# Lower parts by an accumulating DMA in every second weight half, and the retention gate between the token tiles

## What is computed

```
h = rms_norm(x, norm1_w)
q, k, v, g_ret, x_lru, y_lru, gate_ret, gate_lru = split(h @ w_in)
o = chunkwise_retention(rotary(q), rotary(k), v)     # 4 heads of 256
mu, var over each head of o
o = (o - mu) * rsqrt(var + eps) * gn_w               # head_group_norm
y_a = (o * silu(g_ret)) @ w_ret_o
y_b = (rg_lru(conv(x_lru)) * gelu(y_lru)) @ w_lru_o
x = x + (sigmoid(gate_ret) * y_a + sigmoid(gate_lru) * y_b) @ w_out
h = rms_norm(x, norm2_w)
gate, val = split(h @ ffn_w_up)                      # 3072 each
x = x + (gelu(conv3(gate)) * val) @ ffn_w_down
out = rms_norm(x, norm_f_w)
```

## Time and profile before

| | us |
|---|---|
| median of 3 executions | 993.83 (992.47 to 996.0) |
| the profiled execution, its own time | 990.71 |
| its span, first to last instruction | 988.9 |
| TensorE busy in the span | 922.5 |
| GpSimd busy | 440.5, of which L2093 405.1 |
| VectorE busy | 445.3 |
| ScalarE busy | 333.4, of which L1026 139.3 |

### The profile page before, as it was taken

How to read it: one execution, slowest core, us unless ns; L and a number is a source line. 1 busy time by engine, 2 the same in 40 slices (tenths; PEclk the granted TensorE clock), 3 DMA queues, 4 the chain that set the end, 5 groups by cost and what they waited for, 6 DMA issues and landing times.

```text
span 988.9 us, 15018 instructions
## 1 busy us (share of the span) xinstructions
PE 922.5 (93%) x5878; PEld 834.1 (84%) x5878; DVE 445.3 (45%) x951; ACT 333.4 (34%) x636; POOL 440.5 (45%) x561
## 2 busy tenths in 40 slices
PE   4999999999999999999989997799999998999995
PEld 3888888888888776788989997798988998899894
DVE  2284475512588788713592366501122353232132
ACT  3102443102001144504444765243112443443441
POOL 0040000100011000006899689793450798999992
PEclk9999999999999899999999999799999999999998
DMA  8444223143343411332645355252523364555551
GB/s 336 157 149 150 86 86 121 54 157 137 129 170 129 171 43 44 104 124 85 220 144 172 105 198 170 85 188 88 221 75 129 108 190 156 172 185 191 173 189 44
DMA packets 37640, 139.35 MB, mean 141 GB/s; under 512 B 4289, under 2 KB 4289, under 8 KB 37313
## 3 DMA queue, kind: packets, MB, share of 16 engines
q1 hardware_dynamic: 37424, 136.97, 40.1%
q10 hardware_dynamic: 144, 1.41, 0.3%
HBM read 137.32 MB, written 1.05 MB: 140 GB/s over the span
## 4 chain that ended last, share of the span: by engine, by line
PE 65%; POOL 19%; DVE 9%; issue 3%; ACT 2%; DMA 2%; SPq 0%; DVEq 0%; ACTq 0%; POOLq 0%
PE psum L496 35%; POOL w_lo L2093 18%; PE psum L497 7%; PE psum L498 7%; PE psum L499 7%; PE psum L647 2%; PE psum L629 2%; PE psum L640 1%; PE psum L571 1%; DMA w_whole<-in_blocks 1%; DVE head_sums L1989 1%; DVE y_lo L1419 1%; DVE h_rows L1568 1%; PE psum L763 1%; ACT w_hi L1026 1%
## 5 line engine op out<-in xcount | busy, mean ns | idle before, releaser
L2093 POOL TENSOR_TENSOR w_lo<-raw,w_hi 128x256 fp32r<-128x256 f32 x536 | 405.1, 798 | 143.8 <-ACT w_hi L1026 142.8
L496 PE MATMUL psum<-w_whole,h_whole 128*128 128x256 f32 (+1 forms) x960 | 219.6, 382 | 1.9 <-ACT h_whole L1064 1.1
L497 PE MATMUL psum<-h_hi,w_hi 128*128 128x256 f32 x704 | 203.0, 288 | 17.9 <-DVE rows L1983 11.9
L2101 POOL TENSOR_TENSOR rstd<-mean_sq,minus_half 128x2 f32<-128x2 f32 (+4 forms) x20 | 35.1, 1753 | 399.6 <-DVE mean_sq L1429 399.6
L498 PE MATMUL psum<-h_lo,w_hi 128*128 128x256 f32 x704 | 201.7, 287 | 0.0
L499 PE MATMUL psum<-h_hi,w_lo 128*128 128x256 f32 x704 | 201.5, 286 | 0.0
L496 PEld LDWEIGHTS psum<-w_whole,h_whole 128*128 128x128 f32 x960 | 177.6, 192 | 26.5 <-issue 2.8
L1026 ACT ACTIVATE w_hi<-raw 128x1024 fp32r<-128x1024 f32 x136 | 139.3, 1054 | 95.2 <-DMA raw<-in_blocks 68.0
L497 PEld LDWEIGHTS psum<-h_hi,w_hi 128*128 128x128 f32 x704 | 137.6, 195 | 20.4 <-DVE rows L1983 12.1
L498 PEld LDWEIGHTS psum<-h_lo,w_hi 128*128 128x128 f32 x704 | 137.7, 196 | 0.1
L499 PEld LDWEIGHTS psum<-h_hi,w_lo 128*128 128x128 f32 x704 | 137.7, 196 | 0.0
(11 more groups left out here) (276 smaller groups left out, 1260.4 us busy)
## 6 DMA issues: line engine op xcount, KB each, us to landing
raw<-in_blocks SPq DMA_DIRECT2D x136, 512.0 KB, 3.5
w_whole<-in_blocks SPq DMA_DIRECT2D x96, 512.0 KB, 4.4
w_late<-in_blocks SPq DMA_DIRECT2D x20, 512.0 KB, 4.6
early<-in_early SPq DMA_DIRECT2D x1, 1651.0 KB, 7.4
attention<-in_late ACTq DMA_DIRECT2D x1, 1376.0 KB, 7.6
rows<-in_mem SPq DMA_DIRECT2D x2, 512.0 KB, 3.4
x<-in_x SPq DMA_DIRECT2D x1, 1024.0 KB, 9.5
out_x<-h_rows SPq DMA_DIRECT2D x2, 512.0 KB, 2.6
```

What stands on the lines that cost most here:

```text
L496: return nc.tensor.matmul(out, lhs[0], rhs[0], start=start, stop=stop, skip_group_check=shared_bank)
L497: nc.tensor.matmul(out, lhs[0], rhs[0], start=start, stop=False, skip_group_check=shared_bank)
L2093: ins = nc.gpsimd.tensor_tensor(lo[:, at], full[:, at], hi[:, at].bitcast(F32), ALU.subtract)
L2101: rstd_ready.mark(nc.gpsimd.tensor_tensor(rstd[:, n % 2, 0:width], mean_sq[:, n % 2, 0:width], minus_half[:, 0:width], ALU.pow), name, pool)
```

## The change

In every second half (odd j, except the last) the lower part is no longer subtracted by GpSimd. ScalarE writes the negated rounded weight into `w_lo` and the rounded weight into `w_hi`, both from `raw`. GpSimd issues, per quarter, a DMA that reads the quarter again from HBM and adds it onto `w_lo`, so that weight minus upper part stands there when it has landed (`lo_landed`, one semaphore for each quarter of each split slot). TensorE waits for `w_hi_ready` and the two landings instead of `w_lo_ready`. The `raw` slot of such a quarter is free once `w_hi_ready` has counted it. Halves 1, 3, ..., 65 are made so: 33 halves, 66 quarters.

In the retention part the separate scaling of `head_sums` goes: the mean is subtracted by one instruction per token tile that scales and adds. The two halves of the gate `g_ret1` are applied one after each of these instructions instead of both after the mean of the squares.

```
             else:
-                eng.wait_ge(w_lo_ready, 2 * (half_index[half] + 1))
+                j = half_index[half]
+                if lower_by_dma(j):
+                    eng.wait_ge(w_hi_ready, 2 * (j + 1))
+                    for q in (2 * j, 2 * j + 1):
+                        eng.wait_ge(*summed_at(q))
+                else:
+                    eng.wait_ge(w_lo_ready, subtracted(2 * j + 1))
+        def lower_by_dma(j):
+            return j % 2 == 1 and j < len(HALVES) - 2
...
             for q in range(2 * len(HALVES)):
-                if q >= RAW_SLOTS:
-                    sp.wait_ge(w_lo_ready, q - RAW_SLOTS + 1)
+                if q >= RAW_SLOTS and lower_by_dma((q - RAW_SLOTS) // 2):
+                    sp.wait_ge(w_hi_ready, q - RAW_SLOTS + 1)
+                elif q >= RAW_SLOTS:
+                    sp.wait_ge(w_lo_ready, subtracted(q - RAW_SLOTS))
...
                         act.wait_ge(quarter_landed[q % RAW_SLOTS], 16 * (q // RAW_SLOTS + 1))
+                        if lower_by_dma(j):
+                            if j < SPLIT_SLOTS:
+                                slot_left(act, 2 * j + 1)
+                            nc.scalar.activation(split_part(w_lo, q), raw[:, q % RAW_SLOTS, :], ACT.Copy, scale=-1.0)
                         nc.scalar.activation(split_part(w_hi, q), raw[:, q % RAW_SLOTS, :],
                                              ACT.Copy).then_inc(w_hi_ready, 1)
...
-            retention_gate(0)
+            for half in range(2):
+                retention_gate(0, half)
             for h in range(RET_HEADS):
                 settle(xpose, ("ret", h))
-            link(V.tensor_scalar(head_sums[:, :, :], head_sums[:, :, :], -1.0 / S, None, ALU.mult))
             o = h_rows[:, :, :].rearrange("p t (h d) -> p t h d", h=RET_HEADS)
             for t in range(T):
-                link(V.tensor_tensor(o[:, t], o[:, t], spread(head_sums[:, t, :], [P, RET_HEADS, S], 2), ALU.add))
+                link(V.scalar_tensor_tensor(o[:, t], spread(head_sums[:, t, :], [P, RET_HEADS, S], 2), -1.0 / S, o[:, t],
+                                            ALU.mult, ALU.add))
+                retention_gate(1, t)
...
-            r = scale_from("gn", sumsq[:, 0:T * RET_HEADS], S, between=lambda: retention_gate(1))
+            r = scale_from("gn", sumsq[:, 0:T * RET_HEADS], S)
...
                         pool.wait_ge(w_hi_ready, q + 1)
+                        if lower_by_dma(j):
+                            pool.dma_start(split_part(w_lo, q), blocks_d[2 * len(WHOLE) + q],
+                                           accum_op=ALU.add).then_inc(lo_landed[q % (2 * SPLIT_SLOTS)], 16)
+                            continue
```

More of the change, by code:

```diff
@@ L351, in build @@
         w_lo_last = sem("w_lo_last")
+        lo_landed = [sem(f"lo_landed{i}") for i in range(2 * SPLIT_SLOTS)]
         SRC = ([f"x2_{j}" for j in range(4)] + [f"ret_y{j}" for j in range(4)]
@@ L414, in wait_half, with subtracted, summed_at @@
             else:
-                eng.wait_ge(w_lo_ready, 2 * (half_index[half] + 1))
+                j = half_index[half]
[7 more added lines that the diff above has]
+            return j % 2 == 1 and j < len(HALVES) - 2
+        def subtracted(q):
+            return sum(not lower_by_dma(p // 2) for p in range(q + 1))
+        def summed_at(q):
+            turn = sum(lower_by_dma(j) for j in range(q // 2 % SPLIT_SLOTS, q // 2 + 1, SPLIT_SLOTS))
+            return lo_landed[q % (2 * SPLIT_SLOTS)], 16 * turn
         def split_part(w, q):
@@ L1436, in root_of, with scale_from @@
                 return rstd[0:p, n % 2, 0:NORMS[n][1]]
-            def scale_from(name, sums, count, factor=1.0, between=None):
+            def scale_from(name, sums, count, factor=1.0):
                 mean_from(name, sums, count, factor)
@@ L1446, in scale_from @@
                     angles()
-                if between is not None:
-                    between()
                 return root_of(name, sums.shape[0])
@@ L1974, in _, with retention_gate @@
                 decayed(h)
[L1976 to L1984, removed]
-            retention_gate(0)
+            def retention_gate(b, half):
+                n = 2 * b + half
+                use = (f"g_ret{b}", half)
+                arrive(proj, use)
+                vec.wait_ge(g_tanh, n + 1)
+                dst = rows[:, :, 2048 + 512 * b + HC * half:2048 + 512 * b + HC * (half + 1)]
+                proj.freed(V.scalar_tensor_tensor(dst, by_tokens(act_tmp[:, n % 2, :]), 1.0,
+                                                  by_tokens(bank_of(use)), ALU.add, ALU.mult), use, vec)
+            for half in range(2):
+                retention_gate(0, half)
             for h in range(RET_HEADS):
                 settle(xpose, ("ret", h))
-            link(V.tensor_scalar(head_sums[:, :, :], head_sums[:, :, :], -1.0 / S, None, ALU.mult))
             o = h_rows[:, :, :].rearrange("p t (h d) -> p t h d", h=RET_HEADS)
             for t in range(T):
-                link(V.tensor_tensor(o[:, t], o[:, t], spread(head_sums[:, t, :], [P, RET_HEADS, S], 2), ALU.add))
+                link(V.scalar_tensor_tensor(o[:, t], spread(head_sums[:, t, :], [P, RET_HEADS, S], 2), -1.0 / S, o[:, t],
+                                            ALU.mult, ALU.add))
+                retention_gate(1, t)
                 sq = scratch[:, :].rearrange("p (h d) -> p h d", d=S)
```

## The result

The changed kernel takes 1071.11 us (median of 4, 1069.95 to 1074.63) beside 993.15 for the kernel before: ratio 1.080, 95% interval 1.077 to 1.083. It is 78 us slower; the forecast was 17.7 us faster, with a range that ended at 1008. Rival (a), slow adding transfers, is what happened, at more than the price that it was given.

What follows compares the result with a forecast made beforehand. TensorE and GpSimd were taken to run at the same pace, 5.7 us a half. Retention -13.4, GpSimd's relief -12.7 and late DMA halves +8.4 gave -17.7 us, a median near 976, range 965 to 1008.

Steps and rivals of the forecast that it cites:

- Rival (a): Accumulating transfers are slow, TensorE waits in nearly every odd half, kernel slower; about 1033 us at x = 10.5; chance 0.22.
- What bounds the kernel: TensorE and GpSimd run at the same pace, 5.7 us a half; TensorE's waits for GpSimd are 8.4 us.
- The size of x: End of ScalarE's fourth copy to landing of the second quarter: taken as 5.2 us, making FFN halves 8.4 us late.
- The upper bound: Largest x allowed: 7.0 us, twice the 3.5 us plain load, if reading the destination too doubles everything.
- The formula around x: TensorE wants an odd half after 11.4 us; less eviction and copies, x may be 6.4 us, 3.8 in the tight half.
- the gains of 26.1 us: Time saved before DMA costs: 13.4 us in the retention part plus 12.7 us from relieving GpSimd.
- Share of the engines: DMA engines in the FFN: 84% at the plain price, 112% at twice it, then 38 us a step, about 997.
- Retention part: At the block 2 gate, TensorE's 12.1 us stand and 2.8 us of clock go, 1.5 us come back: 13.4 us less.
- Rival (c): VectorE's new scale-and-add is still held by GpSimd, at most 5.7 us; about 981 us; chance 0.12.
- GpSimd's relief: 33 of 67 halves leave GpSimd; TensorE's waits and low clock shrink, 4.9 us at 509-526 us and 7.8 in the FFN: 12.7 us.
- the signs named: Trace signs if right: GpSimd under 240 us busy, no gate wait, one 1 to 2 us wait per FFN step, landings 4 to 6 us.

Runs made afterwards that it cites:

- the copy run: The changed kernel with GpSimd's DMAs copying the quarter onto `w_lo` without adding: 1007.7 us, ratio 1.015.
- the sooner issue: Against the kernel summing only first quarters of odd halves by DMA, GpSimd issues on the negated copy instead of the upper part: 993.97 us, ratio 1.000.
- the DMA part alone: The changed kernel with the retention part of the kernel before: 1066.16 us, ratio 1.073.
- the retention run: The kernel before with only the retention part of the change, every lower part subtracted by GpSimd: 989.13 us, ratio 0.998.

## Why the prediction was wrong

**What bounds the kernel: right.** TensorE and GpSimd keep the same pace, and relieving GpSimd has little to give: 16 us for both parts with the transfers free.

**The size of x: the step that failed.** The prediction took x, from ScalarE's last copy to the landing, at 5.2 us between 3.5 and 7.0. It is 959.8 to 970.8, 11.0 us, in the chain shown; the second quarters land 9.9 us after their issue (median of 33, 5.8 to 11.8). The upper bound, twice the plain landing, was itself too low. By the medians three pieces are in it. A plain first quarter from GpSimd's queue lands in 4.8 us, against 3.5 on SyncE's queue in the kernel before: 1.3 us, of which the share of GpSimd's path and that of the other traffic were not separated. Adding puts 3.4 us on top, 8.2 instead of 4.8, which is inside the 1.6 to 3.5 that the prediction had for a second read; it is more than the engine time shows, which nearly doubles (312 against 163 ns a packet, some 1.3 us for the 144 packets over 16 engines). And the second quarter of a pair lands 1.8 us later after its issue than the first, as in the copy run (2.1 us): the quarters are issued 0.6 to 3.7 us apart, and the second shares the engines with the first. I priced one plain landing of SyncE's queue plus the second read, and neither of the other two pieces.

**The formula around x: right for pairs, too hopeful for single quarters.** The window of 11.4 us, minus copies and eviction, was stated, and with a measured chain of 15.1 us it gives 3.7 us of stand where 3.9 were measured. The rule behind (a stand is what the chain is over 11.4 us, shared between neighbours where every odd half is late) foretold two results: 17 us for a chain 1.05 us shorter (16 expected) and 1064 us for half the DMA halves (1055 to 1080 expected). With single quarters it was too hopeful three times: 996 us against 990, 994 against 981 to 984 with the sooner issue, and 1004 against 983 to 987 with ten of them. There GpSimd's own subtractions hold back many of the issues, which the rule leaves out, and a single quarter lands in 8 to 9 us. At x = 10.5 the rival gave 1033, 38 us under the result. What the sum left out or had too large points that way: x was nearer 11, the clock fell with the longer stands (up to 30 us), and the gains of 26.1 us were at most 16. How the 38 us divide between these was not measured.

**Share of the engines: wrong as a bound.** Rival (a) argued from 112% of the DMA engines. Over two FFN steps their share was 0.79, in a window within a stand 1.04 (as the profile counts it). That they fill up in spurts may lengthen a landing, which no run shows by itself; the halved traffic of the run with every fourth half shows that the sum was not the limit. Its step of 38 us was also short of the 44.6 measured. The rule of the Trainium skill, Collectives: The Full Stack, section The bandwidth ceiling, that an adding transfer reads two sources and runs at half the rate, agrees with the 1.85 of this trace, and with 1.91 against the plain packets of GpSimd's own queue. The fit of the Trainium skill, DMA: Bandwidth & Descriptors, section Anatomy of one DMA, an estimate of 3.2 us, does not cover what was seen: 5.4 us for the plain copy beside other traffic.

**Retention part: wrong by all its gain.** 13.4 us less were expected; alone it gave 0.2%, at most 0.4% or 4 us, and not clear of nothing. The step that failed is that the first scale-and-add takes 1.23 us from 606.06 on. 1.23 us was L1992 beside an idle GpSimd; beside a busy one it was held 11.26 us in the execution traced. Rival (c) had named it, but with a hold of at most one half's run, 5.7 us, on the ground that DMA halves break up GpSimd's runs. In the changed kernel they do (the scale-and-add took 1.31 us beside a run of eight pieces), but there the gain was worth nothing: with the DMA part alone the old order was not held either, 0.26 us, and TensorE did not wait for the gate line. The two gains were added up, though the second one took away what the first was to remove.

**GpSimd's relief: mechanism right, size not separated.** 12.7 us was the sum. Without transfers the FFN has no stand left, as foretold, and both parts together bring 16 us where the retention part alone brought 3; so 12 to 14 us come with the relief, but some of them are the hold at the gate, which that run does not have (its first scale-and-add took 1.34 us). Of the signs named, GpSimd's busy time came out wrong too: 303 us instead of under 240, 57.8 of them its issues.

## What to carry to other kernels

A resource that is relieved on average can be paid for in latency: with three slots and two halves of cover, what counts for a replaced step is its whole chain from the released slot to the landing, against the time that the consumer takes over the slots between. Cost a transfer on the queue that will issue it, beside the traffic that will be there and with its neighbour on the queue, and try a few of its kind before 66 of them. Before taking out an instruction that waited long, ask what it waited for: here the next one waited in its place, and moving the work to an engine outside the conflict (ScalarE) helped, by 7 us. Two gains that remove the same wait must not be added.

## What was not expected of the hardware

- An accumulating DMA of 512 KB (128 rows of 4 KB), HBM onto SBUF, lands 9.0 us after its issue (median of 66), a plain one from the same queue 5.4 us, a plain one from SyncE's queue 3.5 us in the kernel before and 5.9 in the changed one. Mean engine time per packet: 312 ns adding, 163 plain from GpSimd's queue, 169 from SyncE's in the changed kernel. GpSimd itself is occupied 0.89 us by each accumulating issue.
- A single accumulating quarter, with none before it, is not quicker than the first of a pair: 8.7 us after its issue in the run with ten of them and 8.1 in the run with 33, against 8.2 for the first and 9.9 for the second of the pairs (medians).
- VectorE operations on SBUF alone are held by GpSimd's unbroken runs only sometimes. The small scaling took 10.34 us in the kernel before and 0.26 us in the run with the DMA part alone; the scale-and-add 11.26 us in the retention run and 1.3 to 2.5 us beside shorter runs; `y_lo` 9.3 us once in the kernel before (at 809.95 us), and 0.8 to 1.1 us beside the same run of GpSimd and beside the later ones; in the four other kernels without these transfers it is the same one of the twelve that takes 9.3 us. The exclusion that the prediction named for L1989 does not by itself tell these cases apart. Operations with one SBUF and one PSUM input were not held in any of these places (0.69 us each). What decides it stays open.
- GpSimd is slowed in return: eight pieces take 5.6 us where VectorE does no such work and 9.56 us beside its two-input operations.
